# A two-model transformer kernel: rotary angles computed on GpSimd, modulation pieces and compressed-weight flips moved

## The reference, cut to what matters

```
# first block, 2 layers
mod = silu(c) @ w_ada[l] + b_ada[l]                 # 6 x 1024: shift1, scale1, gate1, shift2, scale2, gate2
proj = modulate(rmsnorm(x), shift1, scale1) @ w_in[l]   # 4128 columns for attention + 3072 of gates
q  = rmsnorm(proj[:768]) @ w_uq[l];  kv = rmsnorm(proj[768:1024]) @ w_ukv[l]     # latent projection
# rope (cos, sin of positions * inv_freq) on parts of q and k, then three attentions
x += gate1 * (merged @ w_out);  x += gate2 * (relu(modulate(..., shift2, scale2) @ w_ff1)**2 @ w_ff2)
# second block, 2 layers
proj = rms_norm(x) @ w_in_2[l]
k_cmp, v_cmp = gelu(windows(k, v) @ cmp_w1) @ cmp_w2         # 15 compressed keys and values, 2 groups
p_c = masked_softmax(q @ k_cmp)                              # "compressed weights", 8 heads x 256 x 15
o = g0 * (p_c @ v_cmp) + g1 * (selected attention) + g2 * (window attention)
```

## Time and profile before

| | us |
|---|---|
| median of 3 runs | 1763.9 (1763.39 to 1764.46) |
| the profiled execution | 1765.69 |
| its span | 1764.0 |
| TensorE busy in the span | 1697.8 |
| VectorE | 1180.5 |
| ScalarE | 836.3 |
| GpSimd | 125.9 |

### The profile page before, as it was taken

How to read it: one execution, slowest core, us unless ns; L and a number is a source line. 1 busy time by engine, 2 the same in 40 slices (tenths; PEclk the granted TensorE clock), 3 DMA queues, 4 the chain that set the end, 5 groups by cost and what they waited for, 6 DMA issues and landing times. The chain is left out here.

```text
span 1764.0 us, 24759 instructions
## 1 busy us (share of the span) xinstructions
PE 1697.8 (96%) x9275; PEld 1381.1 (78%) x9275; DVE 1180.5 (67%) x2156; ACT 836.3 (47%) x1473; POOL 125.9 (7%) x271
## 2 busy tenths in 40 slices
PE   6899999999999999999999999999999999999998
PEld 3787676589887796774799878766998787669986
DVE  6787555866866875657745675655788766657885
ACT  3335364355443352652455353464554544645552
POOL 1000011000000000210000010141000100410000
PEclk8999999999999999999999999899999999999999
DMA  9787424557854975326465646604665466036652
GB/s 340 273 292 240 144 82 142 181 190 265 298 177 153 351 265 173 120 96 215 144 217 189 193 143 225 169 1 141 206 183 187 158 215 179 1 121 215 187 184 84
DMA packets 185913, 323.71 MB, mean 184 GB/s; under 512 B 13541, under 2 KB 101185, under 8 KB 185793
## 3 DMA queue, kind: packets, MB, share of 16 engines
q1 hardware_dynamic: 183200, 320.54, 55.8%
q10 hardware_dynamic: 2592, 1.57, 0.3%
HBM read 321.02 MB, written 1.05 MB: 183 GB/s over the span
## 5 line engine op out<-in xcount | busy, mean ns | idle before, releaser
L1747 DVE TENSOR_TENSOR ring_r<-ring,high 128x1024 fp32r<-128x1024 f32 (+3 forms) x382 | 450.6, 1195 | 274.3 <-ACT high L1323 265.8
L1323 ACT ACTIVATE high<-ring 128x1024 fp32r<-128x1024 f32 (+3 forms) x382 | 393.0, 1037 | 483.1 <-PE bank L701 345.7
L701 PE MATMUL bank<-ring_r,featT_r 128*128 128x512 f32 (+3 forms) x864 | 330.5, 383 | 0.0
L701 PE MATMUL bank<-high,featT_r 128*128 128x512 f32 (+3 forms) x680 | 265.8, 391 | 7.2 <-DVE ring_r L1747 4.6
L701 PE MATMUL bank<-featT_r,high 128*128 128x256 f32 x960 | 272.6, 284 | 0.0
L701 PE MATMUL bank<-featT_r,ring_r 128*128 128x256 f32 x960 | 271.6, 283 | 0.0
L701 PE MATMUL bank<-oT_r,high 128*128 128x256 f32 x960 | 271.6, 283 | 0.0
L701 PE MATMUL bank<-high,oT_r 128*128 128x512 f32 (+3 forms) x680 | 258.2, 380 | 0.0
L701 PE MATMUL bank<-high,gates_r 128*128 128x512 f32 x736 | 230.0, 390 | 3.4 <-DVE ring_r L1747 2.6
L701 PEld LDWEIGHTS bank<-featT_r,high 128*128 128x128 f32 x960 | 184.2, 192 | 1.0 <-DVE ring_r L1747 0.7
L701 PEld LDWEIGHTS bank<-oT_r,high 128*128 128x128 f32 x960 | 184.2, 192 | 0.3 <-issue 0.2
(11 more groups left out here) (259 smaller groups left out, 2232.9 us busy)
## 6 DMA issues: line engine op xcount, KB each, us to landing
ring<-in_w_ff SPq DMA_DIRECT2D x128, 512.0 KB, 4.8
ring<-in_w_ada SPq DMA_DIRECT2D x96, 512.0 KB, 5.7
ring<-in_w_up SPq DMA_DIRECT2D x176, 256.0 KB, 3.3
ring<-in_w_in SPq DMA_DIRECT2D x64, 464.0 KB, 5.7
ring<-in_w_in SPq DMA_DIRECT2D x48, 512.0 KB, 5.5
ring<-in_w_in SPq DMA_DIRECT2D x48, 474.0 KB, 4.9
ring<-in_w_down SPq DMA_DIRECT2D x44, 512.0 KB, 3.4
ring<-in_w_out SPq DMA_DIRECT2D x24, 512.0 KB, 5.2
```

The costliest lines, as they stand in the source:

```text
L701: ins = pe.matmul(o, a, b, start=start, stop=stop, skip_group_check=True)
L1323: act.activation(it["high"], it["raw"], ACT.Copy).then_inc(high_ready, 1)
L1747: dve.tensor_tensor(it["low"], it["raw"], it["high"].bitcast(F32), ALU.subtract).then_inc(low_ready, 1)
```

## The change

There are three parts.

The angles go from DVE to POOL, which waits for the positions (`pos_ready`); there they take 25 instructions, since the fused multiply-add of DVE becomes a multiply and a subtraction. ACT takes the sine behind unit 5 rather than 2, and DVE waits for it only ahead of the first rotation.

The 24 modulation steps of layer 0's projection become two beside every unit (20) and four beside w_uq: two ahead of the gate unit's splits, two between the two w_uq results. Part 9 is summed behind the latent projection, part 5 behind unit 4.

In the second block PE flips the hidden ahead of the wait that ends `turns`. The rest of `compressed` moves one step earlier and behind the scores, and the flips of the weights, and ACT's copies of them behind its exponentials, are spread over steps 5 and 6.

```diff
-        IN_STEPS = [[2, 2, 2, 4, 4] + [2] * 5, [0, 4, 4, 4] + [2] * 6]
-        IN_OUT = [{2: 4, 3: 5, 5: 6, 6: 7, 8: 8, 10: 9}, {2: 4, 3: 5, 4: 6, 6: 7, 8: 8, 10: 9}]
+        IN_STEPS = [[2] * 10, [0, 4, 4, 4] + [2] * 6]
+        IN_OUT = [{2: 4, 4: 5, 6: 6, 8: 7, 10: 8}, {2: 4, 3: 5, 4: 6, 6: 7, 8: 8, 10: 9}]
...
                 plain(*[cols_piece(w_uq[l], k0, k0 + 2, (UQ_W * u, UQ_W * u + UQ_W)) for k0 in range(0, QR // P, 2)])
+                for _ in range(0 if l else 2):
+                    ada_piece()
...
+        PAIRS_AT = {5: (0, 2), 6: (1, 3)}
...
-        LATE_AT = 2
+        LATE_AT, SINES_AT = 2, 5
...
+            def angles_of_positions():          # on GpSimd, behind rstd_parts of layer 0
+                pool.wait_ge(pos_ready, 1)
+                for t in range(T):
+                    pool.tensor_scalar(trig[:, 2, 32 * t:32 * t + 24], cst[:, C_INV:C_INV + 24], posc[:, t:t + 1], None, ALU.mult)
...
+                for a, ahead in ((1, 0.0), (0, 0.25)):
+                    link(pool.tensor_scalar(turnsn, trig[:, 2, :], 1 / TWO_PI, ahead, ALU.mult, ALU.add))
...
+                    for part in (PI_A, PI_B, PI_C):
+                        link(pool.tensor_scalar(part_of, turnsn, part, None, ALU.mult))
+                        link(pool.tensor_tensor(trig[:, a, :], src, part_of, ALU.subtract))
+                        src = trig[:, a, :]
...
+                pool.sem_inc(angles, 1)
...
@@ tensor
                 for _ in range(2):
                     linear((for_dve, for_dve), lambda c, t: lat(6 + c)[:, t * P:(t + 1) * P])
+                if l == 0:
+                    modulation(9)
...
+                def hidden_back():
+                    pe.wait_ge(for_act.read, at_act[0])
+                    b, at_act[0] = claim(for_act)
+                    for m in range(4):
+                        flip(b[:, m * 32:m * 32 + GRP * NCMP], gel[:, m * P:(m + 1) * P], for_act.full if m == 3 else None)
-                turns(key_turns + dil_turns)
+                turns(key_turns + dil_turns, hidden_back)
...
-                    elif i == 5:
-                        seen.more(pc_out)
-                        for h2 in range(NSA // 2):
+                    elif i in PAIRS_AT:
+                        if i == 5:
+                            seen.more(pc_out)
+                        for h2 in PAIRS_AT[i]:
...
-                softmax_heads(second_jobs, compressed)
+                softmax_heads(second_jobs, weights_stored, compressed)
@@ scalar
+                    if behind_exps is not None:
+                        behind_exps(i)
                     if i >= 2:
                         for e in range(2):
                             b = tile()
...
@@ vector
-                for t in range(T):
-                    dve.tensor_scalar(trig[:, 2, 32 * t:32 * t + 24], cst[:, C_INV:C_INV + 24], posc[:, t:t + 1], None, ALU.mult)
...
-                dve.sem_inc(angles, 1)
+                dve.sem_inc(pos_ready, 1)
                 seen.more(c_exp, 1)
-                seen.more(sines)
...
                 features_out(pcol[:, l, 16:24])
+                for _ in range(0 if l else 2):
+                    ada_step()
                 split_unit()
...
                     read(for_dve, dve.tensor_copy(qmla[:, 1, u * UQ_W:(u + 1) * UQ_W], b[:, 0:UQ_W]))
+                    for _ in range(2 if u == 0 and l == 0 else 0):
+                        ada_step()
...
+                if l == 0:
+                    modulation_out(l, 9)
```

More of the change, by code:

```diff
@@ L158, in two_blocks @@
         tiny = sb("tiny", [P, 80])
-        stat = sb("stat", [P, 24])
+        stat = sb("stat", [P, 88])
         mx = sb("mx", [P, NSM, T])
@@ L263, in two_blocks @@
         pos_cast = sem("pos_cast")
+        pos_ready = sem("pos_ready")
         angles = sem("angles")
@@ L664, in _ @@
                 rstd_parts(IN_TURN)
+                if l == 0:
+                    angles_of_positions()
                 rstd(12, QR)
@@ L1231, in _ @@
                         owed.append((piece_used, 2))
+                at_act = [n]
+                def hidden_back():
[3 more added lines that the diff above has]
+                        flip(b[:, m * 32:m * 32 + GRP * NCMP], gel[:, m * P:(m + 1) * P], for_act.full if m == 3 else None)
                 seen.more(ready_dve)
-                turns(key_turns + dil_turns)
-                at_act = [n]
+                turns(key_turns + dil_turns, hidden_back)
                 def compressed(i):
                     if i == 0:
[L1239 to L1243, removed]
                         pe.wait_ge(for_act.read, at_act[0])
@@ L1398, in turns_out, with softmax_heads @@
                     read(ins)
-            def softmax_heads(jobs, beside=None):
+            def softmax_heads(jobs, beside=None, behind_exps=None):
                 for i in range(len(jobs) + 2):
@@ L1520, in _ @@
                     if l == 0 and u == LATE_AT:
+                        columns_out((2, 3, 4, 5), (104, 104, 120, 120))
+                    if l == 0 and u == SINES_AT:
                         late_parameters()
@@ L1635, in compressed, with weights_out @@
                         act.activation(pc2[:, :, :, :], pc[:, :, :, :], ACT.Exp).then_inc(pc_exp, 1)
-                    elif i == 5:
-                        for h2 in range(NSA // 2):
+                def weights_out(i):
+                    if i in PAIRS_AT:
+                        for h2 in PAIRS_AT[i]:
                             b = tile()
                             copy_out(pcT[0:NCMP, 2 * h2:2 * h2 + 2, :], b[0:NCMP, :].rearrange("p (h s) -> p h s", s=S))
-                softmax_heads(second_jobs, compressed)
+                softmax_heads(second_jobs, compressed, weights_out)
                 highs(2)
@@ L1995, in late_parameters @@
                 dve.sem_inc(for_dve.read, 1)
-                for t in range(T):
-                    dve.tensor_scalar(trig[:, 2, 32 * t:32 * t + 24], cst[:, C_INV:C_INV + 24], posc[:, t:t + 1], None, ALU.mult)
-                    link(dve.tensor_scalar(trig[:, 2, 32 * t + 24:32 * t + 32], cst[:, C_INV + 24:C_INV + 32],
-                                           posc[:, 2 + t:3 + t], None, ALU.mult))
-                turnsn = tiny[:, 16:80]
-                for a, ahead in ((1, 0.0), (0, 0.25)):
-                    link(dve.tensor_scalar(turnsn, trig[:, 2, :], 1 / TWO_PI, ahead, ALU.mult, ALU.add))
-                    link(dve.tensor_scalar(turnsn, turnsn, ROUNDER, None, ALU.add))
-                    link(dve.tensor_scalar(turnsn, turnsn, -ROUNDER, None, ALU.add))
-                    link(dve.scalar_tensor_tensor(out=trig[:, a, :], in0=turnsn, scalar=-PI_A, in1=trig[:, 2, :], op0=ALU.mult, op1=ALU.add))
-                    for part in (PI_B, PI_C):
-                        link(dve.scalar_tensor_tensor(out=trig[:, a, :], in0=turnsn, scalar=-part, in1=trig[:, a, :], op0=ALU.mult, op1=ALU.add))
-                    if ahead:
-                        link(dve.tensor_scalar(trig[:, a, :], trig[:, a, :], TWO_PI * ahead, None, ALU.add))
-                    link(dve.tensor_scalar(trig[:, a, :], trig[:, a, :], PI_SAFE, -PI_SAFE, ALU.min, ALU.max))
-                dve.sem_inc(angles, 1)
+                dve.sem_inc(pos_ready, 1)
                 seen.more(c_exp, 1)
-                seen.more(sines)
             def cast_positions():
@@ L2121, in _ @@
                        .then_inc(scaled, 1)
+                if l == 0:
+                    seen.more(sines)
                 kpe = proj[:, :, QR + KVR:SB0].rearrange("p t (h e) -> p t h e", h=1)
```

15 lines of the change are left out of this document (12 added, 3 removed).

## The result

The changed kernel takes 1771.0 us (median of 12 runs, 1766.99 to 1772.33) against 1764.75 for the kernel before in the same sessions. The ratio is 1.0031, with an interval of 1.0022 to 1.0040: 5.5 us slower. I forecast 1762.8 and no change. The profiled execution took 1771.39, its span 1769.7, which is 5.7 over that of before.

A forecast was written before the change was run, and what follows sets the result against it. PE, busy 1697.8 of 1764.0 us, was taken as the bound. Terms -7.2, +0.5 and +5.6 sum to -1.1, so the median goes from 1763.9 to 1762.8 us, range 1759.5 to 1766.5, chance 0.52.

The forecast's parts named there:

- the attention: Second block's attention, two layers: later first scores and new stops, less saved waits, +5.6 us; bounds -2.5 to +7.
- Part (c): Second block's attention: savings of 1.9 for waits of 0.47 and 1.70, and 0.3 a layer each for flips and POOL waits.
- The stop of 4.92: First projection, between units 3 and 4: PE's wait for DVE and the slow clock behind it go, -7.2 us.
- GpSimd hides: First projection: POOL's 25 angle instructions take 13 us, at most 26, and end before ACT asks at some 104.
- SP's issue and the end of DVE's splits: Latent projection: the third gate piece is issued at 179.8 and DVE's splits end at 187.7, before the 7.2 shift.
- the first scores start 0.55 later: Second block's attention: `turns` also waits for ACT's copy of the hidden, +0.55 us a layer.
- the stops at steps 5 and 6: Second block's attention: PE stands 1.9 us for weight copies behind ACT's exponentials, twice a layer, 3.8 a layer.
- the latent term: Latent projection: later gate pieces leave 1.3 us of DVE work, less 0.8 for part 9's sum, +0.5.
- rival 2: Second block's attention: the clock falls at step 5's new stops in both layers, 4 us a layer, 1771; chance 0.13.
- rivals 2 and 5: Slower cases: rival 2, and POOL's angles lasting 26 us, holding DVE up by 10, 1768, chance 0.06; together given 0.17.
- the first block up to its `turns`: First projection and latent projection, up to the first `turns`: terms of -7.2 and +0.5 us.

The follow-up runs named there:

- e1: The change's first two parts alone, with the second block's attention of the kernel before; 1758.63 us, ratio 0.9965 against before.
- e3: The changed kernel with the weights' flips ahead of the scores and ACT's copies of them ahead of its exponentials; 1762.59 us, ratio 0.9988 against before.
- e4: The changed kernel, but the wait behind `turns` leaves out the hidden, so first scores don't await its copy; 1766.39 us, ratio 1.0002 against before.
- e5: First two parts, attention of before except the hidden's flips inside the wait behind `turns`, not awaited there; 1757.9 us, ratio 0.9964 against before.
- e9: e7 with the hidden's flips of e5 inside the wait behind `turns`; 1756.86 us, ratio 0.9959 against before.
- e7: e1 with all 24 modulation steps beside the first projection and none beside the latent projection; 1757.31 us, ratio 0.9959 against before.
- e2: The change's third part alone, in the kernel before; 1775.21 us, ratio 1.0058 against before.

## Why the prediction was wrong

The step that failed is the attention: +5.6 forecast, +12.5 measured. Part (c) took off 3.1 for waits that turned out to cost nothing, and the clock over the first scores, 2.65 in the two layers, had no term.

**Right.** The stop of 4.92 and the slow clock behind it go: -7.25 from the fixed start to the flips behind unit 10 with five sums in both, forecast -7.2. GpSimd hides: 17.7 us for 25 instructions, between the 13 and 26 that I bounded from the earlier trace rows, and the sine is asked for at 106.7 (forecast 104). SP's issue and the end of DVE's splits (180.8; forecast 187.7 - 7.2 = 180.5) came out as worked. In the attention, the first scores start 0.55 later a layer, exactly that, and the stops at steps 5 and 6 are 1.99 each against 1.9 forecast, four in all.

**Wrong 1, 0.6 us: the latent term.** I forecast +0.5: 1.3 of DVE's work left over, less 0.8 for part 9's sum that leaves the projection. The two show at different places. Between the flips and the first `turns` it is +2.1 in the changed kernel: DVE's last copy comes 1.4 later (I had 0.8), and part 9's output takes 0.7 to where the rotation starts (I had 0.5). The credit came too, ahead of the flips: the new table has part 8's sum behind unit 10, but one sum fewer in all, 0.95. Together +1.15; over the seven traces with steps there, +0.9 to 1.7.

**Wrong 2, 3.1 us: the credits of the attention, part (c).** I took off 1.9 for the waits of 0.47 and 1.70, 0.6 around the flips and 0.6 for POOL. e1 shows that such a wait is not a cost of its own. Its stage has waits of 0.87, 0.69 and 1.08 that before doesn't have in layer 0, and takes 58.41 against 58.42. Up to the first outputs, PE's waits and its slow clock are two ways to spend the slack in a piece that DVE, ACT and POOL set. Behind them it is the same to see, though no run isolates it: the stage with the wait of 1.70, layer 1 of before, has a "to end" of 38.25, the shortest of the table. e3 took both stops away and put back 1.08 and 1.21, and "to end" went to 39.70 and 39.14, not below the 39.08 and 38.25 of before. Against e1, which differs in the attention alone, "to end" of the changed kernel is 3.99 and 4.04 longer: the two stops of 1.99, in full, and nothing taken off. Against before it is 4.0 and 4.6; my stops less these credits gave 2.25. Of the 4.1 in all that this misses, 3.1 are the credits, 0.4 the stops' 1.99 in place of 1.9, and 0.6 the difference in layer 1 between before (38.25) and e1 (38.84), which run the same attention.

**Wrong 3, 1.15 and 1.5 us: the clock, in the place of the scores.** I held it in rival 2, at 0.13, for the stops of step 5. There it fell as well (slow outputs and scores at 1151.67 and 1153.15), but the lost time of the whole stage is 6.8 in both kernels of layer 0. What differs is where it falls. Before, the slow clock lay from 1137 to 1151, 8 of its 14 us ahead of the first outputs at 1145.30, in the piece with slack. Now the longer wait ahead of the first scores, 1.81, has slow clock right behind it, over the first scores, which head the chain through DVE. DVE's mask of the scores of pair 1, in the changed kernel and then in e1:

```profile
1127.92 0.29 DVE L1977 CUSTOM_DVE_ANT_0 sm<-bank,cst 128x128 f32<-128x128 f32 x1 [1.63 <-PE bank L729]
```

```profile
1125.48 0.29 DVE L1968 CUSTOM_DVE_ANT_0 sm<-bank,cst 128x128 f32<-128x128 f32 x1 [0.58 <-PE bank L729]
```

That is 4.87 and 3.37 behind the first scores, 1.5 apart, and the first outputs are 1.5 apart too: 17.48 and 15.99. Against before: 17.48 and 15.98, and 17.47 and 16.32 in layer 1. That the median came out at the 1771 of rival 2 is chance: its place was another, and a third of its price (2.65 of 8). At the stops of step 5 themselves the slow clock cost nothing to be seen, since "to end" grew by the stops alone. e3's two layers show the price over the first scores with one program: 17.74 with the slow clock there, 15.98 without. e4, with a wait of 0.93, had the first scores at the full clock in both layers (1.55 and 1.55). Whether the wait makes the clock fall there or only makes it likelier, the runs don't settle: without that wait this piece still took 17.23 in e5's layer 1 and 16.60 and 17.22 in e9, there with a slow stretch that starts later and uses up PE's slack.

The sum: -1.1 was forecast for the profiled execution, +5.7 came. Of the 6.8 between them, 6.9 are the attention (6.0 + 6.3, and 0.15 between the layers, against 5.6), and 1.3 the first block up to its `turns` (-5.4 against -6.7), of which 0.6 is its terms and 0.7 the later start of the part that the change touches. Some 1.4 are gained between the first `turns` and the second block's attention, which is within what 13 traces of the same code there differ by. The chances had a slip as well: rivals 2 and 5 add up to 0.19, not 0.17.

The edit to drop is the third part: without it (e1) the kernel is 6.2 us faster than before. The steps beside w_uq should go back as well (e7: 7.2).

## What to carry to other kernels

A wait seen in one trace is a saving only if nothing else sets the end of its stage. Before a wait is counted as gone, add the stage up from a fixed first to a fixed last instruction, and ask which engine's chain gives that length; a slow clock inside the slack of that chain is free until the slack is used up (here at some 4 us lost), and at the head of the chain it costs from the start. A copy out of a bank belongs ahead of the long work of its engine when PE has two banks: behind four exponentials it stopped PE for 2 us each time. And when an edit moves an item across the place that you measure from, count what stands on each side of it, before and after: the same 0.95 us was a gain ahead of the flips and would have looked like a missing credit behind them.

## What the hardware did that I had not expected

POOL's small instructions took 0.24 to 1.38 us for the same 128x64, and DVE's splits beside them kept their 1.12 to 1.17. In the earlier trace rows it was DVE that doubled beside a POOL instruction with two inputs; here POOL gave way. Of POOL's six longest (1.06 to 1.38) five end 0.18 to 0.24 behind the end of a DVE split that started ahead of them or with them, and DVE's 0.82 of the earlier trace rows ends 0.27 behind the two POOL instructions beside it. That one of the two engines waits until the other's instruction has ended fits both places; no run tests it, and which one waits differs between them. The Trainium skill (GPSIMD Engine Reference, 1. Specifications) says that the two share their SBUF interfaces and contend when a VectorE instruction has two SBUF inputs, as the splits have; that section does not say which of the two waits.

The time lost to the clock in the fourteen stages of the table takes only three values, 5.1, 6.8 and 8.5 to 8.6 us. In e2, which the table leaves out, layer 0 has 8.5 too, but layer 1 has 10.3. The same code has one in one layer and another in the next (e3: 8.6 and 5.1), and the time follows where the slow stretch lies at the head of a chain: 17.74 against 15.98.
